# Gate and up products of six FFNs in four arrangements: triples, same-weight pairs, halves of 256 columns by turns, and one half of the sequence first

## The reference, cut to what matters

```python
def swiglu(x, w_gate, w_up, w_down):
    return (jax.nn.silu(x @ w_gate) * (x @ w_up)) @ w_down
```

## Time and profile before

| | |
|---|---|
| median of 3 runs | 3486.01 us (3483.91 to 3487.39) |
| span of the profiled execution | 3480.7 us, and 5.3 us around it to the median of the runs |
| TensorE matmuls | 3359.6 us busy (97%), 14384 of them |
| TensorE weight loads | 2578.8 us (74%), 14384 |
| VectorE | 1595.7 us (46%) |
| ScalarE | 1170.0 us (34%) |
| GpSimd | 411.5 us (12%) |
| mean granted TensorE clock | 0.987 of full |
| chain that ended last | 90% TensorE |

### The profile page before, as it was taken

How to read it: one execution, slowest core, us unless ns; L and a number is a source line. 1 busy time by engine, 2 the same in 40 slices (tenths; PEclk the granted TensorE clock), 3 DMA queues, 4 the chain that set the end, 5 groups by cost and what they waited for, 6 DMA issues and landing times.

```text
span 3480.7 us, 39701 instructions
## 1 busy us (share of the span) xinstructions
PE 3359.6 (97%) x14384; PEld 2578.8 (74%) x14384; DVE 1595.7 (46%) x2295; ACT 1170.0 (34%) x1726; POOL 411.5 (12%) x285
## 2 busy tenths in 40 slices
PE   7999999999999999999899999999999999899998
PEld 5888775778887788876677888565678886668886
DVE  3332489643323433288834331944343327643322
ACT  4332345432323332245533321214333214543322
POOL 1110002111100110000211100400111003111100
PEclk9999999999999999999999999999999999999999
DMA  4333231033333333332023333440223332223332
GB/s 138 93 94 97 85 79 50 3 89 96 91 96 91 90 96 92 95 79 75 1 64 88 96 92 95 99 76 31 65 86 96 93 94 85 61 79 90 96 94 76
DMA packets 420124, 286.04 MB, mean 82 GB/s; under 512 B 57416, under 2 KB 395180, under 8 KB 419884
## 3 DMA queue, kind: packets, MB, share of 16 engines
q1 hardware_dynamic: 419200, 283.62, 28.5%
q10 hardware_dynamic: 828, 1.13, 0.1%
HBM read 280.24 MB, written 4.47 MB: 82 GB/s over the span
## 4 chain that ended last, share of the span: by engine, by line
PE 90%; DVE 6%; ACT 2%; issue 2%; POOL 0%; DMA 0%; DVEq 0%; ACTq 0%; SPq 0%; POOLq 0%
PE bank L856 26%; PE bank L857 26%; PE bank L858 25%; PE bank L851 1%; PE bank L1147 1%; PE bank L1146 1%; PE bank L1165 1%; PE bank L1261 1%; PE bank L1267 1%; PE bank L1384 1%; DVE small L2257 1%; PE bank L996 0%; PE bank L998 0%; PE bank L997 0%; PE bank L1348 0%
## 5 line engine op out<-in xcount | busy, mean ns | idle before, releaser
L858 PE MATMUL bank<-xn_lo,w_hi 128*128 128x512 f32 x2800 | 1097.5, 392 | 0.0
L856 PE MATMUL bank<-xn_hi,w_hi 128*128 128x512 f32 x2496 | 1000.2, 401 | 42.8 <-DVE xn_lo L1973 20.1
L1984 DVE TENSOR_TENSOR w_lo<-wring,w_hi 128x1024 fp32r<-128x1024 f32 x478 | 594.5, 1245 | 926.0 <-ACT w_hi L1511 925.1
L857 PE MATMUL bank<-xn_hi,w_lo 128*128 128x512 f32 x2496 | 989.3, 396 | 0.0
L1511 ACT ACTIVATE w_hi<-wring 128x1024 fp32r<-128x1024 f32 x490 | 517.6, 1059 | 1194.7 <-DMA wring<-in_ffn_down 358.5
L858 PEld LDWEIGHTS bank<-xn_lo,w_hi 128*128 128x128 f32 x2800 | 528.7, 189 | 132.5
L856 PEld LDWEIGHTS bank<-xn_hi,w_hi 128*128 128x128 f32 x2496 | 470.0, 188 | 165.0 <-issue 49.4
L857 PEld LDWEIGHTS bank<-xn_hi,w_lo 128*128 128x128 f32 x2496 | 470.8, 189 | 104.6 <-issue 2.6
L857 PE MATMUL bank<-h_hi,w_lo 128*128 (+1 forms) x1056 | 420.4, 398 | 0.0
L856 PE MATMUL bank<-h_hi,w_hi 128*128 (+1 forms) x1056 | 415.8, 394 | 0.0
L858 PE MATMUL bank<-h_lo,w_hi 128*128 (+1 forms) x1056 | 415.2, 393 | 0.0
(11 more groups left out here) (382 smaller groups left out, 2913.7 us busy)
## 6 DMA issues: line engine op xcount, KB each, us to landing
wring<-in_ffn_gate SPq DMA_DIRECT2D x88, 512.0 KB, 3.8
wring<-in_ffn_up SPq DMA_DIRECT2D x88, 512.0 KB, 3.8
wring<-in_ffn_down SPq DMA_DIRECT2D x88, 512.0 KB, 3.5
wring<-in_ffn_w_gate SPq DMA_DIRECT2D x44, 512.0 KB, 3.8
wring<-in_ffn_w_up SPq DMA_DIRECT2D x44, 512.0 KB, 3.8
wring<-in_ffn_w_down SPq DMA_DIRECT2D x44, 512.0 KB, 3.5
wring<-in_w_in SPq DMA_DIRECT2D x34, 512.0 KB, 3.7
wring<-in_w_out SPq DMA_DIRECT2D x16, 512.0 KB, 3.6
```

The source lines that it names most:

```text
L856: nc.tensor.matmul(ps, w_hi[:, slot, t, 0:M], hi, start=start, stop=False)
L857: nc.tensor.matmul(ps, w_lo[:, slot, t, 0:M], hi, start=False, stop=False)
L858: return nc.tensor.matmul(ps, w_hi[:, slot, t, 0:M], lo, start=False, stop=stop)
L1984: nc.vector.tensor_tensor(w_lo[:, slot, :, :].rearrange("p k c -> p (k c)"), wunit[:, slot, :], w_hi[:, slot, :, :].rearrange("p k c -> p ...
```

## The change

Each FFN gets a form by its number. `triples` is the order of before. `pairs` issues `w_hi` x `xn_hi`, `w_hi` x `xn_lo`, `w_lo` x `xn_hi`, so that two matmuls with the same weights stand next to each other. `weights` splits each matmul into two of 256 columns (HALF = 256), one for each half of the sequence, and issues both halves one after the other with the same weights. `halves` issues all 24 matmuls of a unit for the first 256 tokens, then all 24 for the other 256. Units 0 and 1 of each FFN, all down units, and all other products stay as they are. Waits and signals stay where they were: one per unit.

```diff
+HALF = SEQ // 2
+FFN_FORM = {0: "triples", 2: "pairs", 3: "weights", 5: "halves", 7: "triples", 9: "pairs"}
...
+        def pair_product(ps, slot, t, hi, lo, start, stop):
+
+            nc.tensor.matmul(ps, w_hi[:, slot, t, :], hi, start=start, stop=False)
+            nc.tensor.matmul(ps, w_hi[:, slot, t, :], lo, start=False, stop=False)
+            return nc.tensor.matmul(ps, w_lo[:, slot, t, :], hi, start=False, stop=stop)
+
+        def half_products(bank, slot, halves):
+
+            for k in range(KD):
+                for w, v in ((w_hi, xn_hi), (w_lo, xn_hi), (w_hi, xn_lo)):
+                    for q in halves:
+                        cols = slice(q * HALF, (q + 1) * HALF)
+                        mm = nc.tensor.matmul(pb[bank][:, cols], w[:, slot, k, :], v[:, k, cols],
+                                              start=(k == 0 and w is w_hi and v is xn_hi and q == 0),
+                                              stop=(k == KD - 1 and v is xn_lo), skip_group_check=True)
+            return mm
+
+        def ffn_unit(n, bank, slot):
+
+            if FFN_FORM[n] == "weights":
+                return half_products(bank, slot, (0, 1))
+            if FFN_FORM[n] == "halves":
+                half_products(bank, slot, (0,))
+                return half_products(bank, slot, (1,))
+            product = pair_product if FFN_FORM[n] == "pairs" else split_product
+            for k in range(KD):
+                mm = product(pb[bank][:, :], slot, k, xn_hi[:, k, :], xn_lo[:, k, :], k == 0, k == KD - 1)
+            return mm
...
             def up_unit(bank, m):
                 pe.e.wait_ge(u_lo.h, u0 + m + 1)
-                for k in range(KD):
-                    mm = split_product(pb[bank][:, :], st.slot(m), k, xn_hi[:, k, :], xn_lo[:, k, :], k == 0, k == KD - 1)
-                mm.then_inc(unit_ps.h, 1)
+                ffn_unit(n, bank, st.slot(m)).then_inc(unit_ps.h, 1)
...
-                        for k in range(KD):
-                            mm = split_product(pb[bank][:, :], st.slot(m), k, xn_hi[:, k, :], xn_lo[:, k, :], k == 0, k == KD - 1)
-                        mm.then_inc(unit_ps.h, 1)
+                        ffn_unit(n, bank, st.slot(m)).then_inc(unit_ps.h, 1)
```

## The result

| | before | after |
|---|---|---|
| median of the runs | 3486.29 us (3483.57 to 3487.39, 20 runs) | 3492.19 us (3490.74 to 3494.25, 20 runs) |
| span of the profiled execution | 3480.7 us | 3491.6 us |

The ratio is 1.0020, with a 95% interval of 1.0013 to 1.0026: slower by 5.9 us. The forecast was slower by 37. The two profiled spans lie 10.9 us apart, more than the medians; the clock's part in that is taken up under "What stays open".

What follows compares the result with a forecast made beforehand. TensorE, busy 97% of the span, was taken as the bound, time being matmuls times pitch. Pairs 0, weights +18.6 and halves +18.6 gave a span of 3518 and a median of 3523 us, range 3480 to 3548.

Steps and rivals of the forecast that it cites:

- I take fixed: Split products in n = 3 and 5: each matmul start costs 18.9 ns whatever its width, +37 us; chance 0.57.
- The 18.9: Gate and up loops: ns by which a split product's 232.2 ns pitch exceeds the 213.3 ns of its 512 columns.
- slack in the reading: Plain float32 matmuls and the lower clock: spare reading time hides the extra entirely, given as reason for a per-start cost.
- The proportional rival: Split products in n = 3 and 5: the extra is a rate of reading, +0 to +5 us, 3486 to 3491; chance 0.19.
- The sign: Whole kernel: slower by more than about 7 us has chance 0.72, within it 0.18, faster by more 0.10.
- `pairs` at 0: n = 2 and 9: reordering the three matmuls drops no weight load and changes nothing, 0 us, bounds 10 us either way.
- The load's floor: TensorE: a matmul with a fresh 128 x 128 float32 load comes no faster than 109 ns, or 109 to 112.
- the faster rival: n = 3 and 5: short rows escape the extra and fall to the load's limit, -20 us, 3466; chance 0.09.
- The code rival: n = 3 and 5: the doubled loop body is fetched anew at each jump back, +31 us, 3554; chance 0.07.
- Two passes at half width: n = 3 and 5: 256 columns lose the fast rate and take 215.6 ns, +392 us, 3878; chance 0.03.
- The "mixture" case: n = 3 and 5: the extra is partly per start, partly by rate of reading, 3495 to 3508 us; chance 0.05.
- 5.3 us around the span: Whole run: the profiled span of 3480.7 us lies this far below the runs' median of 3486.0, added to the forecast span.

Runs made afterwards that it cites:

- The scan: Kernel before, gate and up units replaced by 24 equal matmuls at varied start columns and widths of `xn_hi` or `xn_lo`: 3360.61 us beside 3481.51.
- 160 bytes of pad: Kernel before with 40 columns of padding ahead of the buffer that holds `xn_hi`: 3420.17 us against 3485.18, ratio 0.9810.
- the uniform kernels: Changed kernel with one form for all six FFNs, against before at 3485.73 us: `weights` 3516.45, `halves` 3510.84, `pairs` 3485.22 us.
- The loop of four times 128: Kernel before with each FFN's matmuls cut at other columns; the n = 5 loop has four pieces of 128 columns: whole run 3864.85 us.
- without pairs: The change with n = 2 and 9 left as `triples`, against before: 3492.89 us against 3483.66, ratio 1.0026.
- the change again: The unaltered changed kernel measured a second time against before: 3492.75 us against 3484.41, ratio 1.0022.
- alike matmuls: Gate and up units from the third on replaced by 24 equal or alternating matmuls, four sorts in each loop: one run, 3465.85 us.
- 32 bytes of pad: Kernel before with 32 bytes of padding ahead of the buffer that holds `xn_hi`: 3453.99 us against 3484.41, ratio 0.9914.
- 96 bytes of pad: Kernel before with 96 bytes of padding ahead of the buffer that holds `xn_hi`: 3501.81 us against 3484.41, ratio 1.0049.

## Why the prediction was right and wrong

- **The step that failed** is "I take fixed": "106.7 + 18.9 = 125.6 ns; two are 251.2 against 232.2, +18.9 x 1968 = +37 us". The term is 5.6 ns (`weights`) and 4.8 ns (`halves`) by the trace of after, times 984 each 5.5 and 4.7 us; by the sign that the forecast had set itself, a pitch below 120 ns, it is wrong. The scan shows what is in its place: of the 20.0 ns over the columns of `xn_hi` a half has 13.3, two thirds, where fixed asks for all of it. The 18.9 was a mean over two tensors that read at 233 and 227 ns by their places, and it belongs neither to the start alone nor evenly to the columns.
- **The reasons for it.** That slack in the reading "hides the cost entirely" was right as far as it goes: contiguous bf16, half the bytes, shows 2.5 ns. It didn't ask for a fixed cost, though, since a cost by width can hide in the same way. The second, that "the durations differ by a few ns from one matmul to the next of the same size", I read as a sign of a cost by start; it goes with the place. At 160 bytes of pad there is no spread, and `xn_hi` takes 6.7 ns less.
- **The proportional rival** (+0 to +5 us, chance 0.19) was nearest with its upper end. By the rule of the Trainium skill ("TensorE: Matmul & The Clock Gate", section "Back-to-back issue gap") the estimate was 5 us in all; here +5.9. The nearness is of size only: the rule's 215.8 and 109.2 ns are what contiguous bf16 shows, to the tenth, and its whole-and-half difference of 2.5 ns is a third to a half of the 4.8 to 7.4 that split products show.
- **The sign, and `pairs` at 0**, were right: 0.0 us in the loops, 0.9999 with all six so. `weights` and `halves` alike: 0.7 us apart for an FFN in the trace, 0.9 in the runs of the uniform kernels, within the 5 named.
- **The load's floor** was right: 111.5 to 111.7 ns for 128 columns against the 109 to 112 read, and the faster rival falls, since a half stays 7 to 8 ns above it. (The 109 of the plain matmuls with 64 columns holds one first distance of 56 ns; the ones behind it in that stretch are 111.6.)
- **The code rival** falls: no instruction transfer in nine iterations of the doubled body. Of the two statements that the Trainium skill makes ("Runtime: NRT & Kernel Launch", section "Instruction fetch mechanics") this alone can't choose: two lines of 16 KiB with 256 instructions each hold 512, so the 390 of the body need not miss, against what the prediction has. The loop of four times 128 can: its 768 stay over nine iterations too, which fits the 128 KiB for TensorE and not the two lines. (The price of the rival was a little high: two transfers with as much again for asking are 3.7 us, less 2.1 is 1.5 us and not 1.7, so 27 us in place of 31.) **Two passes at half width** falls with the pitch of 118.9. The "mixture" case (0.05), a part by start and a part by width, came nearest to the mechanism, with too high a span.
- **Two readings don't hold.** The earlier trace rows don't show that equal neighbours are loaded anew: `pe_mean` issues four matmuls and leaves eight records each time (22.8 to 26.9 us), so each plain float32 matmul comes as two, with a load each. That `pairs` drops no load is shown by its own 14384 loads. And the "5.3 us around the span" are no constant: in the runs that list both, the time is 1.7 to 2.9 us over the core's span, so the earlier trace rows come from one of the quicker executions. The forecast of the difference doesn't hang on either.
- **The gap before unit 4** shrank with unit 3: 0.14 us, as 24 x 5.6 ns = 0.13 asks. The 0.9 us forecast followed from the wrong pitch.

**What stays open.** The loops of the change add 10.1 us by the trace, the runs 5.9, 9.2 (without pairs) and 8.3 (again): the medians of before lie up to 2.6 us apart between these measurements. From the down stage of n = 3 to unit 2 of n = 5, where nothing was changed, the profile of after is 2.7 us shorter, and the granted clock goes with it. The windows view of the stages from n = 3 to 5 and from n = 7 to 9, each time before, then after; the columns are those of the earlier trace rows, the clock third from the end:

```profile
1479.80:1819.30 339.50, 321.32 (x1455) 231.58 (x1454) 253.06 (x470) 158.65 (x309) 44.60 (x34) 0.97 0.20 52
1486.90:1823.70 336.80, 318.68 (x1454) 228.92 (x1453) 253.16 (x470) 158.53 (x309) 44.83 (x34) 0.98 0.20 53
...
2877.10:3096.10 219.00, 189.68 (x714) 138.03 (x713) 142.52 (x170) 105.34 (x142) 46.80 (x22) 0.94 0.24 70
2887.20:3107.40 220.20, 190.70 (x715) 138.50 (x713) 143.08 (x170) 105.33 (x142) 47.05 (x23) 0.92 0.24 70
```

The first stage has 17.1 us at 1.2 GHz before and 10.2 after, the second 27.3 and 34.1. The timed runs show the same: beside "the change again" those of before have a mean of 3483.1 us at a granted clock of 0.987, 3484.8 at 0.986 and 3486.7 at 0.984, those of the change 3491.5 at 0.987 and 3493.0 at 0.986. At equal clock the change costs 8.5 and 8.2 us. So a part of the scatter in the differences is how much of each run fell to the lower clock; why that differs from run to run isn't shown, and 2 us between these and the 10.1 stay open.

The weights were never moved, so it isn't shown that their common place matters and not the absolute one. And the pitches of alike matmuls don't add up to every mix: 2 x 233.3 + 226.7 = 693.3 ns, where before has 696.7, 32 bytes of pad 686.7, 96 bytes 703.3; only at 160 bytes do they agree (680.0). What makes the extra, and what the place has to do with it, isn't shown.

## What to carry to other kernels

When matmuls run back to back, divide their pitch by the columns at the granted clock first, and measure the remainder at two widths and two start places before costing a split: it may be neither per instruction nor per byte. Look where in its partition the moving tensor starts: a pad of 160 bytes, which put it at the same place modulo 256 bytes as the weights, was worth 1.9% of this kernel and cost nothing. Don't cut a product away from its middle when the small piece is below the floor of the weight load (111 ns here for 128 columns).

## What the runs showed of the hardware that was not expected

- A matmul of 512 float32 columns in fp32r has a pitch of 226.7 to 234.1 ns at full clock by where its moving columns start; 213.3 is the columns' own time.
- The extra over the columns grows with the width, but not evenly: 13.3 ns at 256 columns, 11.7 at 288, 16.7 at 384, 20.0 at 512 (13.4 at the best place).
- One column repeated 512 times comes at 218.7 ns; two-byte values that lie 4 bytes apart at 226.5, contiguous at 215.8.
- Equal weights for 24 matmuls in a row don't make them faster: 233.1 to 233.4 ns, alike and alternating.
- A loop body of 384 matmuls and 384 weight loads runs nine iterations without an instruction transfer.
- The time of an unchanged stage moves with its share at the lower clock: 339.5 us with 17.1 us at 1.2 GHz, 336.8 with 10.2.
